# Retention scores in a hybrid decoder layer: one masked matmul per four heads, or one matmul per head in the four row groups of the array

## The reference, cut to what matters

```python
qc = q.reshape(B, N, C, H, dk)      # C = 128 tokens, H = 8, dk = 32
kc = k.reshape(B, N, C, H, dk)
vc = v.reshape(B, N, C, H, dv)      # dv = 64
scores = jnp.einsum('bnchd,bnmhd->bnhcm', qc, kc) * inner_decay
inner = jnp.einsum('bnhcm,bnmhe->bnche', scores, vc)
kv = jnp.einsum('bnchd,hc,bnche->bnhde', kc, k_decay, vc)
...
    return chunk_decay[None, :, None, None] * state + kv_i, state
...
cross = jnp.einsum('bnchd,nbhde,hc->bnche', qc, prev_states, q_decay)
out = (inner + cross).reshape(B, S, H, dv).astype(jnp.float32)
```

## Time and profile before

| | |
|---|---|
| median of 3 runs | 2466.48 us (2464.45 to 2466.92) |
| the profiled execution, its own time | 2464.76 us |
| its span, first to last instruction | 2462.8 us |
| mean granted TensorE clock | 0.989 |
| PE busy over the span | 2402.1 us (98%) |
| DVE, ACT, POOL busy | 58%, 38%, 26% |
| mixing stage | about 850 to 1165 us of the span |

### The profile page before, as it was taken

How to read it: one execution, slowest core, us unless ns; L and a number is a source line. 1 busy time by engine, 2 the same in 40 slices (tenths; PEclk the granted TensorE clock), 3 DMA queues, 4 the chain that set the end, 5 groups by cost and what they waited for, 6 DMA issues and landing times. The chain is left out here.

```text
span 2462.8 us, 35231 instructions
## 1 busy us (share of the span) xinstructions
PE 2402.1 (98%) x12048; PEld 2030.9 (82%) x12048; DVE 1429.7 (58%) x2671; ACT 928.0 (38%) x1790; POOL 628.6 (26%) x397
## 2 busy tenths in 40 slices
PE   7999999999999989999899999989999999999998
PEld 6888888889999968887688888878888887888887
DVE  4332346625555567778756656775666655455655
ACT  4301122217777613234433333533333343332332
POOL 0099455525554467763000000000000000000001
PEclk9999999999999989999999999999999999999999
DMA  5413224476777445555433333433334335445655
GB/s 188 132 64 112 69 82 115 113 188 167 177 179 180 142 144 167 182 172 192 134 99 106 94 119 106 124 111 102 106 94 119 106 105 206 141 141 194 236 206 187
DMA packets 309033, 344.91 MB, mean 140 GB/s; under 512 B 17216, under 2 KB 240064, under 8 KB 308672
## 3 DMA queue, kind: packets, MB, share of 16 engines
q1 hardware_dynamic: 308928, 343.55, 45.9%
HBM read 231.41 MB, written 112.07 MB: 139 GB/s over the span
## 5 line engine op out<-in xcount | busy, mean ns | idle before, releaser
L1816 PE MATMUL fin_psum_bank<-ff_b_hi,ff_w_hi 128*128 128x512 f32 x1232 | 482.7, 392 | 18.3 <-issue 8.6
L1816 PE MATMUL fin_psum_bank<-ff_b_lo,ff_w_hi 128*128 128x512 f32 x1232 | 482.2, 391 | 0.0
L1816 PE MATMUL fin_psum_bank<-ff_b_hi,ff_w_lo 128*128 128x512 f32 x1232 | 481.8, 391 | 0.0
L2115 POOL TENSOR_TENSOR ff_ssq<-ff_ssq,ff_minus_half 128x1 f32<-128x1 f32 x16 | 14.8, 925 | 1269.2 <-DVE ff_ssq L2383 1269.2
L1816 PEld LDWEIGHTS fin_psum_bank<-ff_b_hi,ff_w_hi 128*128 128x128 f32 x1232 | 233.0, 189 | 69.0 <-issue 9.0
L1816 PEld LDWEIGHTS fin_psum_bank<-ff_b_hi,ff_w_lo 128*128 128x128 f32 x1232 | 233.0, 189 | 48.8
L1816 PEld LDWEIGHTS fin_psum_bank<-ff_b_lo,ff_w_hi 128*128 128x128 f32 x1232 | 232.9, 189 | 48.2
L1898 PE MATMUL fin_psum_bank<-ff_down_hi,ff_act_hi 128*128 128x512 f32 x616 | 240.5, 390 | 3.7 <-DVE ff_act_lo L2147 3.7
L1898 PE MATMUL fin_psum_bank<-ff_down_lo,ff_act_hi 128*128 128x512 f32 x616 | 240.3, 390 | 0.0
L1898 PE MATMUL fin_psum_bank<-ff_down_hi,ff_act_lo 128*128 128x512 f32 x616 | 240.2, 390 | 0.0
L2119 DVE TENSOR_TENSOR ff_w_lo<-ff_raw,ff_w_hi 128x512 fp32r<-128x512 f32 x176 | 120.9, 688 | 145.9 <-ACT ff_w_hi L1909 145.9
(11 more groups left out here) (207 smaller groups left out, 4635.4 us busy)
## 6 DMA issues: line engine op xcount, KB each, us to landing
ff_act_raw<-a_parts SPq DMA_DIRECT2D x56, 704.0 KB, 4.1
ff_raw<-in_w_gate SPq DMA_DIRECT2D x22, 1024.0 KB, 6.0
ff_raw<-in_w_up SPq DMA_DIRECT2D x22, 1024.0 KB, 5.3
a_parts<-ff_a_sum SPq DMA_DIRECT2D x88, 256.0 KB, 6.0
ff_down_raw<-in_w_down SPq DMA_DIRECT2D x77, 256.0 KB, 4.7
a_parts<-ff_up SPq DMA_DIRECT2D x66, 256.0 KB, 2.3
att_out<-at_orow SPq DMA_DIRECT2D x192, 66.0 KB, 2.8
mx_att_in<-att_out SPq DMA_DIRECT2D x16, 792.0 KB, 4.8
```

Source lines behind the costliest of these rows:

```text
L1816: last = nc.tensor.matmul(to, w[:, i, k, :], b[i][:, k, :], start=fresh and k == 0 and which == 0, stop=k == KH - 1 and which == 2, skip_g ...
L2115: nc.gpsimd.tensor_tensor(ssq[:, n % 2, 1:2], ssq[:, n % 2, 1:2], minus_half[:], ALU.pow).then_inc(rooted, 1)
```

## The change

POOL no longer spreads the queries; `q_heads`, `head_rows` and the semaphore `q_ready` go. PE does one matmul per head instead of one per unit: the head's 32 rows of keys as weights (32 x 128), the head's 32 rows of queries (128 columns) as the moving operand, placed in the row group in which these rows lie (`tile_position`). The four heads of a unit go to four banks. The banks are laid out anew: heads to banks 1 to 4 (the two units side by side in each), `kv_ps` to bank 4, `o_ps` to bank 5. Bank 1 is shared with the second half of `tp`, and bank 4 with `kv_ps`, so two waits are new: the scores wait for the previous chunk's `kv_masked`, and `turn_mix` waits for both units' `probT` where it waited for `k_done`. The key transposes move to the first two slots of `tp` (bank 0). DVE waits once for all scores of a chunk where it waited for each unit.

```diff
-    q_heads = [place(f"q_heads{i}", [P, NU, HU, P], frame((16, 15)[i])) for i in range(2)]
-    head_rows = place("head_rows", [P, HU], NARROW + 128)
-    s_ps = bank[:, 2:4, :].rearrange("p u (h q) -> p u h q", q=P)
-    o_ps = bank[:, 4, :].rearrange("p (h e) -> p h e", e=RET_DV)
-    kv_ps = bank[:, 5, :].rearrange("p (u e) -> p u e", u=NU)
+    s_ps = bank[:, 1:1 + HU, 0:NU * P].rearrange("p h (u q) -> p u h q", q=P)
+    kv_ps = bank[:, HU, :].rearrange("p (u e) -> p u e", u=NU)
+    o_ps = bank[:, HU + 1, :].rearrange("p (h e) -> p h e", e=RET_DV)
...
-            for tile, name in ((head_rows, "head_rows"), (q_decay, "q_decay"), (k_decay, "k_decay")):
+            for tile, name in ((q_decay, "q_decay"), (k_decay, "k_decay")):
...
-    def by_head(pool, c, s):
+    def decayed(pool, c, s):
         wait_loaded(pool, qkv_loaded[s], c, s, 3)
-        if not isinstance(c, int) or c > 1:
-            pool.wait_ge(S["scored"], 2 * c - 2)
-        for u in range(NU):
-            q = qkv[:, s, u, :].unsqueeze(1).broadcast_to([P, HU, P])
-            rows = head_rows[:].unsqueeze(2).broadcast_to([P, HU, P])
-            nc.gpsimd.tensor_tensor(q_heads[s][:, u], q, rows, ALU.mult).then_inc(S["q_ready"], 1)
...
                 if on(0):
                     pe.wait_ge(S["k_done"], c + 1)
+                    pe.wait_ge(S["prob_done"], 2 * c + 2)
...
-                    last = nc.tensor.transpose(tp[:, 4 + u, :], qkv[:, s, 2 + u, :], ident[:])
+                    last = nc.tensor.transpose(tp[:, u, :], qkv[:, s, 2 + u, :], ident[:])
                 last.then_inc(S["turned"], 1)
+                if later(c):
+                    pe.wait_ge(S["prob_done"], 2 * c)
+                    pe.wait_ge(S["kv_masked"], c)
                 for u in range(NU):
-                    pe.wait_ge(S["q_ready"], 2 * c + u + 1)
-                    if later(c):
-                        pe.wait_ge(S["prob_done"], 2 * c + u - 1)
-                    nc.tensor.matmul(s_ps[:, u], qkv[:, s, 2 + u, :], q_heads[s][:, u], start=True, stop=True).then_inc(S["scored"], 1)
+                    for h in range(HU):
+                        at = slice(h * RET_DK, (h + 1) * RET_DK)
+                        last = nc.tensor.matmul(s_ps[:, u, h], qkv[at, s, 2 + u, :], qkv[at, s, u, :], start=True, stop=True,
+                                                tile_position=(h * RET_DK, 0), skip_group_check=True)
+                last.then_inc(S["scored"], 1)
...
-                nc.vector.tensor_tensor(k_dec[:], tp[:, 4:6, :], k_decay[:], ALU.mult).then_inc(S["k_done"], 1)
+                nc.vector.tensor_tensor(k_dec[:], tp[:, 0:NU, :], k_decay[:], ALU.mult).then_inc(S["k_done"], 1)
+
+                dve.wait_ge(S["scored"], c + 1)
                 for u in range(NU):
-                    dve.wait_ge(S["scored"], 2 * c + u + 1)
```

More of the change, by code:

```diff
@@ L982, in values @@
         return qkv[:, s, 4:8, :].rearrange("p k q -> p (k q)")
-    names = ("waited consts w_split w_hi_split zeroed turned k_done q_ready q_dec_ready "
+    names = ("waited consts w_split w_hi_split zeroed turned k_done q_dec_ready "
              "scored prob_done output kv_done kv_masked state_done squared var_sum var_done "
@@ L993, in mix @@
     late_consts, gains_loaded, w_loaded = m.sem("late_consts"), m.sem("gains_loaded"), m.sem("w_loaded")
-    CONSTS = 4
+    CONSTS = 3
     bounds = {}
@@ L1129, in early_vector @@
             nc.vector.tensor_copy(w_hi[:, k, :], w_out[:, k, :]).then_inc(S["w_hi_split"], 1)
-    def by_head(pool, c, s):
+    def decayed(pool, c, s):
         wait_loaded(pool, qkv_loaded[s], c, s, 3)
-        if not isinstance(c, int) or c > 1:
-            pool.wait_ge(S["scored"], 2 * c - 2)
-        for u in range(NU):
-            q = qkv[:, s, u, :].unsqueeze(1).broadcast_to([P, HU, P])
-            rows = head_rows[:].unsqueeze(2).broadcast_to([P, HU, P])
-            nc.gpsimd.tensor_tensor(q_heads[s][:, u], q, rows, ALU.mult).then_inc(S["q_ready"], 1)
-    def decayed(pool, c, s):
         if later(c):
@@ L1154, in early_gpsimd @@
         pool.wait_ge(S["consts"], 16 * CONSTS)
-        by_head(pool, 0, 0)
         decayed(pool, 0, 0)
@@ L1464, in step @@
             if opening:
-                by_head(pool, c + 1, 1 - s)
                 decayed(pool, c + 1, 1 - s)
@@ L2512, in constants @@
     row = np.arange(P)[:, None] // RET_DK
-    c["head_rows"] = (row == np.arange(4)[None]).astype(np.float32)
     c["head_cols"] = (row == np.arange(4 * RET_DV)[None] // RET_DV).astype(np.float32)
```

## The result

The changed kernel takes 2450.94 us in the median of 7 runs (2445.01 to 2453.74), the kernel before 2464.45 us in the median of 7 (2456.71 to 2466.92). The ratio is 0.9948, with a 95% interval from 0.9934 to 0.9962: 0.5% faster. A second set of both (5 runs beside 11) gave 0.9937 (0.9924 to 0.9950). The profiled execution took 2451.15 us, its span is 2449.3 us.

The account below looks back on a forecast made before the run. PE, busy 98% of the span, was taken as the bound. Loop -5.6 and opening -0.2 gave -5.8 us: 2459.0 against the profiled 2464.76, plus 1.7 for the median, 2460.7, rounded to 2460.5; range 2455 to 2474.

Parts of the forecast that it names:

- POOL's part is worth nothing: Mixing loop: removing POOL's spreading of the queries, 35.4 us of its work, gains nothing by itself.
- The columns are as many, only row groups can gain: Scores on PE: 16 x 128 x 2 columns against 4 x 512 x 2, so only work in several row groups gains.
- The score phase, 0.96 us for the records: Scores in each loop step: a head's second record follows its first but overlaps the next head's, 9 x 0.107 us.
- my lower end: Scores in each loop step: four row groups fully side by side, four records each, 4 x 0.107 = 0.43 us.
- the pace of L1229: Upper bound for the scores: loads set 0.105 us per record, as in L1229's 8 records, so 16 take 1.71 us.
- Two changes of layout, 0.33 to 0.55, 0.33 taken: Each step: array goes from 128 rows to 32 and back, running empty at 0.16 us each, more if loads cannot run ahead.
- No step can save more than about 0.7: Loop step: L1284 waits for the low part of L1398, slack 0.72 us, so a saving of 0.43 goes through whole.
- 13 steps: Mixing loop: steps 3 to 15 each save 0.43 us, 5.6 us in all.
- `turn_mix`'s and `kv_masked`'s waits unfelt in the loop: New waits in the loop: `turn_mix` has slack 1.09 us, `kv_masked` is over 5 us ahead of the scores.
- The opening, -0.2 with 2 us either way: Steps 0 to 2 of the mixing stage: net saving of 0.2 us, with a possible shift of 2 us either way.
- my signs of being wrong: Signs: 32-row records every 0.1 us without overlap, `turn_mix` waiting for `probT`, or a changed clock in steps 1 and 2.
- rival 1: Scores fully side by side, 0.43 us or little more; L1398 caps saving at 0.7 a step; about 2456.5 us; chance 0.20.

Follow-up runs that it names:

- Eight full-array matmuls: Kernel before with each unit's score matmul split into one per head, 128 rows, old banks, no row groups; 2462.5 us (1 run).
- half the scores: Changed kernel without unit 1's four score matmuls, DVE using unit 0's scores for both; 2448.89 us (1 run); with mean moved too, 2443.68 us (1 run).
- mean moved: Changed kernel with DVE's mean for the last norm put ahead of the five small operations of the softmax weights; 2449.36 us (5 runs), ratio 0.9943.
- four changes of layout: Changed kernel with unit 1's key transpose put between the two units' scores, so the array changes layout four times a step; 2454.52 us (1 run).

## Why the prediction was wrong

- *POOL's part is worth nothing*: right in the loop, where the kernel that keeps it has a period of 17.34; for the whole kernel no difference shows.
- *The columns are as many, only row groups can gain*: right. Eight full-array matmuls cost 0.07 us more than two.
- *The score phase, 0.96 us for the records*: this is the step that failed. I had the heads' records in program order, so that a head's second record holds back the next head's first. They go four at a time: 0.43 us, my lower end, 0.53 less than I took. The period fell by 0.80 where I had 0.43, and 13 x 0.37 = 4.8 us is the greater part of the 7.7 us by which the saving was missed. The loads too run four at a time; the pace of L1229 was a pace of full loads and no bound.
- *Two changes of layout, 0.33 to 0.55, 0.33 taken*: the mechanism was right, and the size is 0.43 with the loads that can't run ahead, 0.10 more than taken. Together 1.29 forecast for the phase from the first score to `out_half(0)`, 0.86 measured.
- *No step can save more than about 0.7*: right in kind, since half the scores gain only 0.03 more. The cap was set 0.1 too low: I took the slack from the load at 1019.33, but that load had run ahead of PE's own work. Where PE waits, the time from the load to the next step is 0.13 shorter (6.45 against 6.58). The cap cost little: PE saved 0.86 and the period 0.80, and with the chain out of the way (mean moved) the period saves 0.83. The last 0.03 is not explained.
- *13 steps*: right; 13 x 0.80 = 10.4 us, where 13 x 0.43 = 5.6 was forecast.
- *`turn_mix`'s and `kv_masked`'s waits unfelt in the loop*: right; the first is met 0.34 us ahead of the load. In step 1 PE does wait for `kv_masked`, 1.55 us, in time that was idle anyway.
- *The opening, -0.2 with 2 us either way*: +1.8 in that profile, +1.6 in the means of the few. The clock, which I had named, did change, and a change in steps 1 and 2 was one of my signs of being wrong. I had it change in step 1; it changed in step 0 already. Why is not shown. PE stands idle 0.79 us behind the short score phase there, but in the profile with four changes of layout, with as many scores, the granted clock was 0.76 over the products of step 0 (853.35 to 860.35) and not 0.50, and its opening was still 46.3 us. And half the scores leave PE even less busy, with openings of 44.4 and 44.5. So the longer opening goes with the change, and the clock as its cause is argued only.

So rival 1 was nearly the truth for the loop. It gave 2456.5 with the opening at -1, and what came was 2450.94. Some 2 us of the distance are the base: I had added 1.7 to the profiled 2464.76, and the kernel before ran at 2464.45 beside the changed one. The saving itself was forecast as 5.8 and measured as 13.5. The loop and step 15 explain 10.4 of 13.5 us in the first set and of 15.4 in the second. As a ratio 10.4 us are 0.9958, which the first interval holds (0.9934 to 0.9962) and the second does not (0.9924 to 0.9950). The other 3 to 5 us lie, in the profiles, in the end of the stage and in the feed-forward block, where the instructions are the same in both kernels and the stretches at 1.2 GHz fall differently. That they are due to the clock alone was not shown, and why they should favour the changed kernel in the medians stays open.

Whether four banks are needed, or heads in one bank would run as fast, was not tried.

## What to carry to other kernels

Matmuls with 32 rows to contract can be placed four at a time, one in each row group, each group with a bank of its own. Here they then cost a quarter of their time each, loads included, in both orders tried; price them by row group, and add about 0.2 us for each change between this layout and the full array (0.43 for the first two, 0.36 for two more). A saving on the busiest engine is worth only the slack of the next chain, so measure where that chain ends and not where a load that may run ahead begins. To find the next limit, take half of the work out, with and without the suspected chain shortened.

## What the runs showed of the hardware that was not expected

- Loads of 32-row weights start in fours, within 0.02 us of each other. With the four records of one head first in the program, within 0.04 us, and eight loads had still started within 0.16 us.
- DVE's operation on 128 x 1024 elements (the normalised row) takes 2.05 us when a multiplication of 128 x 512 on POOL started 0.07 us before it, and 1.28 us when POOL's started 0.16 us after it; then POOL's takes 2.02 us and not 1.04. With POOL idle DVE's takes 1.28 us too (at 1164.33 in the changed kernel).
- Two profiles of the changed kernel have openings of 47.4 and 45.8 us, with the granted clock at 0.50 in 23.90 us of both and then in 6.80 us of the first (880.20 to 887.00) and 3.40 us of the second (877.80 to 881.20), while the loop at full clock repeated to 0.1 us in 208.
